# Gate and up projections of a SwiGLU layer by 7 block products in place of 8, the hidden activations kept in DRAM, and the weights rounded by ScalarE

## What is computed

```python
FFN_HIDDEN = 2816
x = x + g1 * (merged @ w_out[l])
h = rmsnorm(x, norm2_g[l]) * (1.0 + sc2) + sh2
f_gate, f_up = jnp.split(h @ w_ffn_in[l], 2, axis=-1)      # (2048,1024) @ (1024,5632)
x = x + g2 * ((jax.nn.silu(f_gate) * f_up) @ w_ffn_out[l]) # (2048,2816) @ (2816,1024)
return rmsnorm(x, final_g)
```

## Time and profile before

| | |
|---|---|
| median of 3 runs | 2914.86 us (2912.85 to 2917.11) |
| the profiled execution: its time | 2912.66 us |
| its span, first to last instruction | 2910.8 us |
| PE busy | 95% of the span |
| POOL, DVE, ACT busy | 57%, 42%, 18% |
| mean granted clock of PE | 0.98 |

### The profile page before, as it was taken

The page is one execution under the profiler, slowest core; times in us unless marked ns, Lnnn a source line. Parts: engine busy times, 40 slices in busy tenths (PEclk is TensorE's granted clock), DMA queues, the critical chain, the costliest instruction groups (busy, mean ns, idle before and its releaser), DMA issues.

```text
span 2910.8 us, 33340 instructions
## 1 busy us (share of the span) xinstructions
PE 2764.5 (95%) x12295; PEld 2225.4 (76%) x12295; DVE 1214.7 (42%) x1564; ACT 522.2 (18%) x731; POOL 1666.1 (57%) x953
## 2 busy tenths in 40 slices
PE   4778999999999999999999999999999999999998
PEld 1357878877887778787888877888788887888876
DVE  6709852895459653975222212112222212121221
ACT  2210232123210431023111110111101111011120
POOL 3245555645564655655566656666566665666664
PEclk9889999999999999999999999999999999999999
DMA  7484535753373427452533324333244332343322
GB/s 247 159 226 129 160 102 154 179 152 100 123 202 113 152 87 199 134 166 80 197 99 94 94 92 157 120 94 94 90 135 142 94 100 87 122 152 94 101 87 79
DMA packets 489048, 377.45 MB, mean 130 GB/s; under 512 B 90408, under 2 KB 418296, under 8 KB 488824
## 3 DMA queue, kind: packets, MB, share of 16 engines
q1 hardware_dynamic: 377088, 289.44, 32.9%
q10 hardware_dynamic: 111864, 86.75, 10.2%
HBM read 336.23 MB, written 31.46 MB: 126 GB/s over the span
## 4 chain that ended last, share of the span: by engine, by line
PE 74%; DVE 14%; issue 3%; ACTq 3%; DMA 2%; ACT 2%; POOL 1%; DVEq 0%; POOLq 0%
PE bank L1222 16%; PE bank L1223 16%; PE bank L1224 16%; PE bank L1387 5%; PE bank L1389 5%; PE bank L1388 5%; DVE bank L681 3%; PE bank L1329 2%; PE bank L1331 2%; PE bank L1330 2%; DVE wst L730 1%; PE bank L1284 1%; PE bank L1285 1%; DVE bank L708 1%; DVE wst L710 1%
## 5 line engine op out<-in xcount | busy, mean ns | idle before, releaser
L1222 PE MATMUL bank<-h_hi,w_hi 128*128 128x512 f32 x2304 | 904.2, 392 | 28.0 <-ACT uz L980 18.3
L1223 PE MATMUL bank<-h_lo,w_hi 128*128 128x512 f32 x2304 | 899.1, 390 | 0.0
L1224 PE MATMUL bank<-h_hi,w_lo 128*128 128x512 f32 x2304 | 899.1, 390 | 0.0
L1483 POOL TENSOR_TENSOR w_lo<-raw,w_hi 128x1024 fp32r<-128x1024 f32 x264 | 638.5, 2419 | 21.1
L1481 POOL CAST w_hi<-raw 128x1024 fp32r<-128x1024 f32 x264 | 281.0, 1064 | 534.9 <-PE bank L1224 329.0
L1465 POOL CAST w_hi<-raw 128x1024 fp32r<-128x1024 f32 x192 | 220.2, 1147 | 567.9 <-PE bank L1224 463.8
L1222 PEld LDWEIGHTS bank<-h_hi,w_hi 128*128 128x128 f32 x2304 | 434.5, 189 | 126.0 <-ACT uz L980 18.7
L1224 PEld LDWEIGHTS bank<-h_hi,w_lo 128*128 128x128 f32 x2304 | 434.2, 188 | 91.4
L1223 PEld LDWEIGHTS bank<-h_lo,w_hi 128*128 128x128 f32 x2304 | 434.4, 189 | 88.9
L1467 POOL TENSOR_TENSOR w_lo<-raw,w_hi 128x1024 fp32r<-128x1024 f32 x192 | 485.1, 2526 | 15.4
L828 DVE TENSOR_TENSOR bank<-bank,tr 128x512 f32<-128x512 f32 x88 | 61.5, 699 | 720.8 <-PE bank L1224 681.5
(11 more groups left out here) (231 smaller groups left out, 2810.0 us busy)
## 6 DMA issues: line engine op xcount, KB each, us to landing
raw<-in_w_ffn_in SPq DMA_DIRECT2D x176, 512.0 KB, 3.8
raw<-in_w_in SPq DMA_DIRECT2D x112, 512.0 KB, 4.7
raw<-in_w_ffn_out SPq DMA_DIRECT2D x88, 512.0 KB, 3.7
ada<-in_w_ada SPq DMA_DIRECT2D x24, 1024.0 KB, 5.2
ssm_m<-vk_scratch SPq DMA_DIRECT2D x32, 512.0 KB, 4.6
raw<-in_ssm_glu SPq DMA_DIRECT2D x32, 512.0 KB, 3.3
raw<-in_w_out SPq DMA_DIRECT2D x32, 512.0 KB, 3.8
xs<-x_scratch ACTq DMA_DIRECT2D x20, 512.0 KB, 11.5
```

What stands on the lines that cost most here:

```text
L1222: t.matmul(dst, wh, xh, start=first, stop=False)
L1223: t.matmul(dst, wh, xl, start=False, stop=False)
L1224: return t.matmul(dst, wl, xh, start=False, stop=last)
L1483: g.tensor_tensor(lo[:], src[:], hi[:].bitcast(F32), ALU.subtract).then_inc(split_done, 1)
```

## The change

**Block products.** A pair `q` is one gate tile and the up tile beside it, for a group of 1024 tokens (two blocks). The 22 pairs run for group 0 and then for group 1, 44 in all (`N1`). The weights of a pair are the 2x2 blocks A11, A12 (gate, first and second half of the contraction), A21, A22 (up); the activations are B11, B12, B21, B22 (half of the contraction, half of the tokens). Strassen's scheme in Winograd's form makes the four results from seven products of 4 x 3 = 12 matmuls each, where the plain form has eight. It needs four sums of weights S1 to S4 for each pair, four sums of activations T1 to T4 for each group, and seven sums of products for each pair.

**Engines.** Product `i` goes to bank `i`. For each pair POOL makes 4 sums (`w_sum`) and 7 remainders (`w_low`) of 128x512, each a tensor_tensor; ACT rounds the 7 weights of the next pair (`w_high`), copies product 0 (`copy_product`) and applies silu twice; DVE makes 7 sums (`sum_of`) out of PSUM and 2 products (`hidden`). ACT writes product operands of the next pair into the same slot, once the product before has read it.

**Activations.** T1 to T4 and their splits (`x_sum`, `x_high`, `x_low`, each in two halves of 128x1024) are made at the start of group 0 and, for group 1, inside pair 21, the last of group 0 (`ending` in the code). The rows of group 1 are loaded, normalised and transposed in pairs 12 to 19 (`load_rows`, `turn_rows`, `stage_rows`: two pairs for each two row tiles). The second block of group 0 is normalised and transposed inside the last call of `mixers` (`last=True`): four more squares and a square root on ACT, four scalings on DVE, and 32 transposes on PE (`second_half`) after chunks of `o0` and `o1`. DVE's residual step of `o1` moves behind the first activation sums (`last_residual(1)` at pair 0).

**Hidden tiles** are stored unrounded to DRAM by SP (`store_pair`, 256 KB each). Then the output layer runs for all four blocks with the same 2112 matmuls: hidden tiles are loaded again, rounded by ACT (`hid_high`) and split by DVE (`hid_low`) into a ring of 24; banks 0 to 3 and 4 to 7 take turns between the two column halves. POOL splits the weight chunks as before. The hardware loops of the feed-forward part are gone; all of it is written out.

The core of the diff (the norm of the rows and the output layer are left out; `g, n = divmod(q, NPAIR)`):

```diff
+    NG = SEQ // (2 * TB)
+    NPAIR = KF
+    PRODUCTS = ["B11", "T1", "T2", "B21", "T3", "B22", "T4"]
+    WEIGHTS = ["A11", "S1", "S2", "A12", "S3", "S4", "A22"]
...
+        slot_at = {"B11": uc_at, "T1": uc_at + 16384, "T2": ssm_at + 8192, "B21": ssm_at + 24576,
+                   "T3": end_kept, "B22": mc_at, "T4": ms_at}
...
+        ORDER = [["T1", "T2", "T3", "B22", "T4"], PRODUCTS]
+        SUMS = ["T1", "T2", "T3", "T4"]
...
+            def x_sum(g, name):
+                a, b_ = {"T1": ("B12", "T1"), "T2": ("B22", "T2"), "T3": ("B22", "B12"), "T4": ("B21", "T4")}[name]
+                for half in R(2):
+                    if name == "T1":
+                        dve.wait_ge(stage_done, (4, 40)[g])
+                        if g == 0:
+                            dve.wait_ge(*vec.after("mix", NB - 1, f"hl{KH - 1}"))
+                        else:
+                            dve.wait_ge(xlo_done, xcount(g, "B11", half))
+                    elif name == "T2":
+                        dve.wait_ge(stage_done, (8, 40)[g])
+                        dve.wait_ge(xlo_done, xcount(g, "T1", half))
+                    elif name == "T4":
+                        dve.wait_ge(xlo_done, xcount(g, "T2", half))
+                    v.tensor_tensor(staged(name, half), staged(a, half), staged(b_, half), ALU.subtract)\
+                        .then_inc(xsum_done, 1)
+            def x_low(g, name):
+                for half in R(2):
+                    dve.wait_ge(xhi_done, xcount(g, name, half))
+                    v.tensor_tensor(halves(xc_lo[name], half), staged(name, half),
+                                    halves(xc_hi[name], half).bitcast(F32), ALU.subtract).then_inc(xlo_done, 1)
+            def sum_of(q, n, dst, product_, other, i):
+                dve.wait_ge(product_done, 7 * q + i + 1)
+                if n:
+                    dve.wait_ge(sum_done, 7 * q + n)
+                v.tensor_tensor(dst[:], product_[:], other[:], ALU.add).then_inc(sum_done, 1)
+            def hidden(q, c):
+                dve.wait_ge(gate_done, 2 * q + 1 + c)
+                dve.wait_ge(sum_done, 7 * q + (7, 5)[c])
+                v.tensor_tensor(tr[c][:], bank[(6, 1)[c]][:], tr[c][:], ALU.mult).then_inc(hid_done, 1)
+            x_sum(0, "T1")
+            x_low(0, "T1")
+            x_sum(0, "T2")
+            x_low(0, "T2")
+            x_sum(0, "T3")
+            for q in R(N1):
+                g, n = divmod(q, NPAIR)
...
+                if q == 0:
+                    x_low(0, "T3")
+                    x_low(0, "B22")
+                    last_residual(1)
...
+                if ending:
+                    x_low(g + 1, "B11")
+                    x_sum(g + 1, "T1")
+                dve.wait_ge(copy_done, q + 1)
+                sum_of(q, 0, fsum2, bank[2], fcopy, 2)
+                sum_of(q, 1, fsum4, bank[1], fsum2, 2)
+                if q == 0:
+                    x_sum(0, "T4")
+                    x_low(0, "T4")
...
+                if ending:
+                    x_low(g + 1, "T1")
+                    x_sum(g + 1, "T2")
+                sum_of(q, 2, bank[3], bank[3], fcopy, 3)
+                sum_of(q, 3, fsum2, bank[4], fsum2, 4)
+                sum_of(q, 4, bank[1], bank[1], fsum2, 4)
+                if ending:
+                    x_low(g + 1, "T2")
+                    x_low(g + 1, "B21")
+                    x_sum(g + 1, "T3")
+                sum_of(q, 5, bank[5], bank[5], fsum4, 5)
+                hidden(q, 1)
+                if ending:
+                    x_low(g + 1, "T3")
+                    x_low(g + 1, "B22")
+                sum_of(q, 6, bank[6], bank[6], fsum2, 6)
+                hidden(q, 0)
...
+            def hid_low(*tiles):
+                for n in tiles:
+                    dve.wait_ge(hid_hi_done, n + 1)
+                    v.tensor_tensor(hid_lo[n % RING][:], hraw[n % 4][:], hid_hi[n % RING][:].bitcast(F32),
+                                    ALU.subtract).then_inc(hid_lo_done, 1)
...
+            def x_high(g, name):
+                for half in R(2):
+                    if name in SUMS:
+                        act.wait_ge(xsum_done, xsum_count(g, name, half))
+                    if g:
+                        act.wait_ge(product_done, 7 * (g * NPAIR - 1) + PRODUCTS.index(name) + 1)
+                    elif name in ("B22", "T4"):
+                        act.wait_ge(*tensor.after("mix", NB - 1, f"o1{TT - 1}"))
+                    s.activation(halves(xc_hi[name], half), staged(name, half), ACT.Copy).then_inc(xhi_done, 1)
+            def w_high(q, i):
+                name = WEIGHTS[i]
+                if name[0] == "A":
+                    r = 2 * (q % 2) + int(name[1]) - 1
+                    act.wait_ge(fraw_in[r], 16 * (q // 2 + 1))
+                    src = fraw[r][:, (int(name[2]) - 1) * KH * P:int(name[2]) * KH * P]
+                else:
+                    act.wait_ge(wsum_done, 4 * q + int(name[1]))
+                    src = fsum[int(name[1]) - 1][:]
+                if q:
+                    act.wait_ge(product_done, 7 * (q - 1) + i + 1)
+                elif i >= 3:
+                    act.wait_ge(*tensor.after("mix", NB - 1, "oc1" + str(KD // 2 - 2) if i < 5 else f"o1{TT - 1}"))
+                s.activation(fw_hi[i][:], src, ACT.Copy).then_inc(whi_done, 1)
+            def copy_product(q):
+                act.wait_ge(product_done, 7 * q + 1)
+                if q:
+                    act.wait_ge(sum_done, 7 * (q - 1) + 3)
+                s.activation(fcopy[:], bank[0][:], ACT.Copy).then_inc(copy_done, 1)
+            def gate_silu(q, c):
+                act.wait_ge(sum_done, 7 * q + (3, 6)[c])
+                if q:
+                    act.wait_ge(hid_out[c], 16 * q)
+                s.activation(tr[c][:], bank[(3, 5)[c]][:], ACT.Silu).then_inc(gate_done, 1)
...
+                ahead = (lambda i: w_high(q + 1, i)) if q + 1 < N1 else (lambda i: None)
+                copy_product(q)
+                ahead(0)
+                if ending:
+                    x_high(g + 1, "B11")
+                ahead(1)
+                if ending:
+                    x_high(g + 1, "T1")
...
+            def product(q, i):
+                g, n = divmod(q, NPAIR)
+                name = PRODUCTS[i]
+                if n == 0:
+                    if g == 0 and name in ("B11", "B21"):
+                        pe.wait_ge(*vec.after("mix", NB - 1, f"hl{KD - 1}"))
+                    else:
+                        pe.wait_ge(xlo_done, xcount(g, name, 1))
+                pe.wait_ge(wlo_done, 7 * q + i + 1)
+                if q == 0:
+                    pe.wait_ge(*vec.after("mix", NB - 1, f"ob{i // 4}{i % 4}"))
+                    pe.wait_ge(stage_done, KD)
+                else:
+                    read = {"B11": (copy_done, q), "T1": (hid_done, 2 * q - 1), "T2": (sum_done, 7 * q - 6),
+                            "B21": (gate_done, 2 * q - 1), "T3": (sum_done, 7 * q - 3), "B22": (gate_done, 2 * q),
+                            "T4": (hid_done, 2 * q)}
+                    pe.wait_ge(*read[name])
+                for j in R(KH):
+                    cols = slice(j * P, (j + 1) * P)
+                    ins = three(bank[i][:], fw_hi[i][:, cols], fw_lo[i][:, cols], xc_hi[name][:, j, :],
+                                xc_lo[name][:, j, :], j == 0, j == KH - 1)
+                ins.then_inc(product_done, 1)
...
+                part = {"A11": gate[:, 0:KH * P], "A12": gate[:, KH * P:], "A21": up[:, 0:KH * P],
+                        "A22": up[:, KH * P:]}
+                for n in R(4):
+                    part[f"S{n + 1}"] = fsum[n][:]
+                def w_sum(name, a, b_, op):
+                    g.tensor_tensor(part[name], part[a], part[b_], op).then_inc(wsum_done, 1)
+                def w_low(i):
+                    pool.wait_ge(whi_done, 7 * q + i + 1)
+                    g.tensor_tensor(fw_lo[i][:], part[WEIGHTS[i]], fw_hi[i][:].bitcast(F32), ALU.subtract)\
+                        .then_inc(wlo_done, 1)
+                if q:
+                    pool.wait_ge(wlo_done, 7 * q)
+                w_sum("S1", "A21", "A22", ALU.add)
+                w_low(0)
+                pool.wait_ge(wsum_done, 4 * q + 1)
+                w_sum("S2", "S1", "A11", ALU.subtract)
+                w_low(1)
+                pool.wait_ge(wlo_done, 7 * q + 2)
+                w_sum("S3", "A11", "A21", ALU.subtract)
+                w_low(2)
+                pool.wait_ge(wsum_done, 4 * q + 2)
+                pool.wait_ge(wlo_done, 7 * q + 3)
+                w_sum("S4", "A12", "S2", ALU.subtract)
+                for i in R(3, 7):
+                    w_low(i)
...
+            def load_pair(q):
+                for up in R(2):
+                    r = 2 * (q % 2) + up
+                    if q >= 2:
+                        sp.wait_ge(wlo_done, 7 * (q - 1))
+                    elif r < RAW:
+                        sp.wait_ge(split_done, NB * NMIX + r + 1)
```

(5 more changed lines are left out.)

634 lines of the change are left out of this document (430 added, 204 removed).

## The result

The changed kernel takes 2871.43 us, the median of 4 runs (2870.26 to 2873.13), beside 2915.67 for the kernel before in the same comparison: a ratio of 0.985 with an interval of 0.9833 to 0.9867. It is faster by 1.5%. Forecast were 2856 us and a range of 2806 to 2888. The profiled execution took 2870.26 us, its span is 2868.1.

A forecast was written before the change was run, and what follows sets the result against it. PE's matmul count was taken to bound the feed-forward layer. Terms -98.1 - 3.5 - 14.9 + 48.5 + 2.6 + 3.2 + 5 = -57.2 took the span from 2910.8 to 2853.6, so 2856 us measured, range 2806 to 2888.

The forecast's parts named there:

- T3: Pair 0, product 4: PE waits for the activation sum T3, delayed by DVE and POOL taking turns; about 7.8 us.
- T4: Pair 0, product 6: PE waits for T4, whose rounding stands behind S1 and S2 work in ACT's queue; 12.8 us.
- four turned rows: Group 1's rows, turned after product 0 before DVE has scaled them: four waits of 2.5, together 10.1 us.
- pair 22: Product 1 of pair 22 waits for DVE's work overloaded in pair 21: 15.3 us, and 2.6 more follow.
- The rival of seams that hide: Group starts and ends: little contention between DVE and POOL, seams 19 us, one or no clock loss; 2823, chance 0.16.
- keeps its 491.0: Output layer: its 2112 matmuls take 491.0 us as before, since POOL needs 3.45 of 5.58 us a chunk.
- 14.9 of old waits: Old feed-forward layer: waits left over beside matmuls and transposes, taken to go with the loops; -14.9 us.
- The matmuls, -98.1: Products: 3696 matmuls at 0.2325 us replace 4224, 957.4 becoming 859.3; the other end, at the old pace, -119.5.
- The seams, +48.5: Pairs 0, 21, 22 and group 1's turned rows: PE waits with DVE and POOL taking turns; 18.9 without turns.
- The rival in which POOL sets the pace: Pairs: POOL limits from 1.77 us an operation on; at 1.96 the kernel is slower, 2978; chance 0.06.
- The clock, +5: Behind three long PE waits, matmuls run at the lower clock, 1.7 us lost each; between 0 and 12.
- The mixers and their end, +6.1 with the transposes: Mixers: 32 added transposes and +2.6 us (0 to 8) for staging and scalings; first product starts at 1428.1, before 1422.0.

The follow-up runs named there:

- e6: Changed kernel with POOL's weight sums and remainders in pairs 0, 1, 21 and 22 replaced by memsets, so those tiles are not fully computed; 2850.13 us, one execution.
- m1: Separate kernel on zeros: matmul series by place and bank change, all 0.2267 us each; DVE's 128x1024 subtraction alone 1.15 us, beside POOL's tensor_tensor 2.08.
- e2: Changed kernel with ACT's rounding of T4 for the first group moved ahead of pair 1's late weights; 2865.38 us, ratio 0.9817.
- e5: Changed kernel with PE's first turning of the rows of each pair of row tiles after product 1 instead of product 0; 2857.76 us, ratio 0.9795.
- e4: Changed kernel with output-layer loads reordered: `x3` behind the first hidden roundings, two hidden loads per weight chunk; 2853.73 us, ratio 0.9786.
- m2: Separate kernel on drawn numbers: fourteen series of 120 matmuls with operands shifted by some bytes and different orders of use; 27.21 to 28.00 us a series.
- m3: m2 with the order of its series reversed and all else the same; 27.22 to 27.99 us a series.
- v_align: Changed kernel with e2, e4, e5 and the second seam's sums spread (2829.48 us together), plus only tile addresses shifted; 2808.5 us, ratio 0.962.
- e1: Changed kernel with the DRAM scratch of the hidden tiles declared behind all others; 2872.17 us, median of four runs from 2861.54 to 2873.39.

## Why the prediction was right, and where it was off

**Right.** PE sets the pace and POOL has idle time in each pair. Its 128x512 took 1.30 us in the steady pairs against 1.26 (1.34 to 1.36 in the mean of its two costliest groups over the whole kernel, seams included), and 148.5 us of 200 are 14.3 of a pair's 19.3; the point of 1.77 is far off. The four kinds of wait stand where the layout put them: 6.3 for 7.8 (T3), 9.6 for 12.8 (T4), 8.2 for 10.1 (four turned rows), 12.8 for 15.3 (pair 22). e6 and m1 show the reason given for two of them, T3 and pair 22, DVE and POOL taking turns; e2 shows ACT's order for T4, and e5 that the turned rows came too early for DVE. The rival of seams that hide (2823) falls with the waits themselves, 36.9 and not 19, and e6 shows why: without POOL's reads DVE takes 1.22, beside them 2.1 to 2.3.

**Off, five terms.**
- *The output layer "keeps its 491.0"*: the matmuls did, 2112 x 0.2322 = 490.4. I checked POOL's time a chunk and `hid_low`, and no DMA queue: hidden tiles, `x3` and weight chunks share SP's and ACT's queues, and three waits, 11.4 us from start to start, and 5.8 of clock came from their order; e4 gives back 15.4 of it. This is the step that failed, with the largest error. 2.4 more are DVE's last scalings behind the last matmul, which the earlier trace rows had counted as the layer's end and which I took away with the "14.9 of old waits".
- *The matmuls, -98.1*: the value for the pace came from the wrong reason, height in SBUF and change of bank; m1 refutes both. The measured term is 847.1 - 957.4 = -110.3, between the two ends kept. m2, m3 and v_align show that it is the distance of the operands' starts. That 0.2325 lay within 1.4% of the 0.2292 measured was luck.
- *The seams, +48.5*: 36.9 and the small gaps of 4.0. The four waits are 16 to 25% shorter than said, and the 2.6 behind pair 22 did not come. Missing was the reverse of the turns: beside DVE's SBUF work POOL took 2.1 to 2.3 an operation, and in pair 0 it set PE's pace for three products. The rival in which POOL sets the pace held for some 13 us in 900.
- *The clock, +5*: 11.3 in phase 1 and 5.8 in the output layer. I charged the three long waits and not the turned rows' of 2.0 us, three of which brought the lower level too, nor any in the output layer.
- *The mixers and their end, +6.1 with the transposes*: +11.9. The last block gave 4.6. The 7.3 come from the first block, at the lower clock behind a wait for a load; e1 has executions of one kernel with and without them, and whether the change makes them more frequent is open.

The first, fourth and fifth are +19.4, +6.3 and +5.8 (the clock of the output layer is within the first), the others -12.2 and -7.6, with +2.8 of small remainders: +14.5. So the total came closer than its terms: 34.3 too low against 19.8 too high, and that they cancel by more than half is luck.

The rule of the Trainium skill that the prediction set beside its rows (SBUF — State Buffer, "Who interferes with whom") is borne out by m1: a tensor_tensor with both inputs in SBUF is held up by GpSimd's reads, 1.15 against 2.08, and with a PSUM input it isn't. Without it the seams were said to be some 30 shorter; e6 measures 15.3 of waits and 4.0 of small gaps. The same skill gives 215.7 ns from start to start for warm matmuls of 512 columns (TensorE: Matmul & The Clock Gate, "Wait — 56ns, not 53.3ns?"). No row here reaches that: 226.7 on zeros, 226.8 at the best distance on drawn numbers, 233.3 at the worst.

## What to carry to other kernels

Removing matmuls paid for what PE then did not wait for: 528 fewer gave 110 us and 44 arrived. Count for each stage not only the engines but the order of each DMA queue, with what stands ahead of the load that PE needs next; two such orders cost some 15 us here. Where PE waits in the midst of full work, add the matmuls at the lower clock behind the wait (here between 0 and some 2.6 us each time), and where DVE must work out of SBUF in a row, keep POOL's reads away or spread it. And look at the start addresses of the two operands before counting a pace: 192 and 128 bytes of free space were worth 19 us.
